# Expert rows in groups of 72 instead of 80 in a hybrid encoder step with 32 experts

## Chip, cores and metric

The kernel runs on one core of a Trainium2 chip. The metric is device time in microseconds of one launch. All data is float32.

## What is computed

One layer of a streaming encoder for 512 prompt tokens and 64 sample tokens, 576 rows of 1024 values: a mixer (SSD and S5 scans), cross attention over 256 memory tokens, and a mixture of experts. The change touches the last of these alone:

```python
def hmoe(x, p):
    """Two-level routing per token: top-1 expert group, then top-2 experts inside it."""
    t = x.reshape(bsz * L, D_MODEL)
    g_logits = (t @ p["w_router_group"]) + p["b_router_group"]
    g_idx = jnp.argmax(g_logits, axis=-1)
    ...
    top_v, top_i = lax.top_k(e_logits, TOP_K_INNER)
    gates = jax.nn.softmax(top_v, axis=-1) * g_prob[:, None]
    ...
    for e in range(N_EXPERTS):
        hid = jax.nn.silu(t @ p["w_gate"][e]) * (t @ p["w_up"][e])
        out = out + (hid @ p["w_down"][e]) * combine[:, e:e + 1]
```

There are 32 experts. Each has a gate and an up matrix of 1024 x 256 and a down matrix of 256 x 1024, 1 MB each. Each of the 576 tokens goes to two experts, so the experts have 1152 rows of work in all. Counted with the reference's routing on its inputs, the experts 0 to 31 get 18, 19, 9, 30, 20, 14, 25, 23, 28, 29, 29, 28, 31, 25, 33, 25, 52, 51, 32, 31, 62, 59, 33, 26, 49, 47, 46, 54, 46, 60, 52 and 66 rows.

## The kernel before

Every engine's program is written out by hand, with semaphores between the engines; nothing is scheduled by a tool. The mixer, the attention and the routing come first. Routing gives each row a rank within its expert (0, 1, 2 ...) and stores the normed rows in the DRAM tensor ffn_rows.

CAP = 80 is the number of row slots of an expert in one pass. The tile slot_id holds for each slot the rank that it takes, filled by GpSimd's iota in DEAL steps (lines 835 to 837):

```python
for turn_ in range(DEAL):
    step(pool.iota(iot[:, turn_:CAP:DEAL], [[1, CAP // DEAL]], base=turn_ * (CAP // DEAL), ...
```

With CAP = 80 and DEAL = 5, slots 0, 5, 10 ... 75 take ranks 0 to 15, slots 1, 6, 11 ... take ranks 16 to 31, and so on. One-hot tables made from it and a product over all tokens (slot_table, line 1377) give gather_index and scatter_index: for each slot and expert the token row to read, and the row of expert_rows to write. Empty slots get an index out of bounds, which moves no row. If an expert had more than CAP rows, overflow_flag would be set, and all engines would run further passes over all experts.

In the pass over the experts (lines named in the functions below), for expert n:
- **GpSimd** gathers the slots' rows into xg (region_r, two buffers, line 862) two experts ahead, once VectorE and TensorE have turned what the buffer held; and it scatters the finished rows yo (line 878). Both are indirect DMAs with CAP slots.
- **TensorE** turns half of xg by products with ident (turn_x, line 918 through turn), **VectorE** the other half (turn_half, line 2352), always in blocks of 32 rows up to 96. The result xgT is in region_t.
- **TensorE** computes gate and up (gate_up, line 1422): the weights are stationary, 64 columns at a time, and CAP columns of xgT stream. One expert has 128 instructions, 64 for each of gate and up. Then it turns the next expert's xg and computes the down product of the one before (down_rows, line 1438): hidden strips of 32, 32 and CAP - 64 rows are stationary, 256 columns of weights stream.
- **ScalarE** applies Silu (line 1801) and evicts (1796, 1809, 1810); **VectorE** multiplies to hidden (1854), and evicts (2379, 2380).
- **SyncE** loads weights (load_part, line 678). There are five sets of buffers for gate, up and down, spread over weight_ring, region_g, region_t, conv_io, act_a and act_b. All five are loaded ahead, during attention and routing. Each of the other 27 experts' sets is loaded into the buffers of the expert four before it: gate and up once that expert's up product is done, down once its down product is. Expert 31 takes the set of expert 0. All of this is one queue, in order.

At the end, each token's two rows are read back from expert_rows, added with their gates, normed and stored.

Of the kernel before, what the change touches and what calls it, by code (L numbers as in the profile page):

```python
# [42 lines left out]
CONV_OUT = CONV_COLS - 3  # L43
SAMPLE_COL = NP + 3
XC = [0, 128, 256, 384, SAMPLE_COL]
CAP = 80
DEAL = 5 if CAP % 5 == 0 else 4
DB = 32
XS = 96
PASSES = -(-T // CAP)  # L50
SETS = 5
# [166 lines left out]
def build(nc, a, o):  # L218
# [14 lines left out]
    with ExitStack() as ctx:  # L233
# [57 lines left out]
        def view(reg, off, *shape):  # L291
            n = 1
            for s in shape:
                n *= s
            v = reg[:, off:off + n]
            if len(shape) == 2:
                return v.rearrange("p (a b) -> p a b", a=shape[0])
            if len(shape) == 3:
                return v.rearrange("p (a b c) -> p a b c", a=shape[0], b=shape[1])
            if len(shape) == 4:  # L300
                return v.rearrange("p (a b c d) -> p a b c d", a=shape[0], b=shape[1], c=shape[2])
            return v
# [58 lines left out]
        xgT = [view(reg_t, XS * KD * i, KD, XS) for i in range(2)]  # L361
        gact = [view(reg_t, 2 * XS * KD + 160 * i, 2, CAP) for i in range(2)]
        hid = [rows[:, 1, 160 * i:160 * i + 2 * CAP].rearrange("p (j l) -> p j l", j=2) for i in range(2)]

# [17 lines left out]
        before = passing.take(NT, NE)  # L382
        oh = [passing.take(NT, CAP) for _ in range(2)]
        r_w = passing.take(NE)
# [9 lines left out]
        prio = lasting.take(NE)  # L394
        slot_id = lasting2.take(CAP)
        tok = [lasting2.take(NT, 2) for _ in range(2)]
# [2106 lines left out]
```

How the kernel before makes its waits and increments, by code:

```python
        def wait_filled(eng, *key):  # L484
            eng.wait_ge(filled, job[key] + 1)
            return bank_of(*key)
# [1 line left out]
        def wait_emptied(eng, *key):  # L489
            who, n = rank[job[key]]
            eng.wait_ge(emptied[who], n)
# [24 lines left out]
        def wait_chunk(eng, c):  # L517
            eng.wait_ge(ring_loaded[c % SLOTS], 16 * (c // SLOTS + 1))
# [43 lines left out]
        def wait_expert_chunk(eng, part, n, i, p):  # L563
            s = set_of(n)
            eng.wait_ge(WSEM[s][part], 16 * LOADS[s] * p + 16 * i + 16 * (WDENSE[s, part] + load_no(n) + 1))
# [1 line left out]
        def overflow_passes(eng, run_pass):  # L568
            eng.wait_ge(flag_ready, 1)
            over = eng.value_load(flag[0:1, 0:1], min_val=0, max_val=1)
            with eng.If(over > 0):
                with eng.Fori(1, PASSES) as p:
                    run_pass(p)
# [6 lines left out]
        @block.sync  # L581
# [47 lines left out]
            sp.dma_start(b_rt[:, 0:NG], a["b_router_group"].rearrange("o g -> (o g)").partition_broadcast(P))\  # L629
              .then_inc(route_loaded, 16)
            sp.dma_start(b_rt[:, NG:], a["b_router_expert"].rearrange("o g e -> (o g e)").partition_broadcast(P))\
              .then_inc(route_loaded, 16)
            sp.wait_ge(tap_ready, 1)
            sp.wait_ge(T_zero, 1)
            for k in range(8):
# [4 lines left out]
            for c in range(CH_GLU, CH_GLU + SLOTS):  # L641
                if c == CH_GLU + 4:
                    sp.wait_ge(h_ready, 1)
                    load_rows(5)
# [111 lines left out]
            def sync():  # L756
                pool.wait_ge(pstep, n[0])
```

## Time and profile before

| | us |
|---|---|
| median of 3 runs | 872.96 |
| the three runs | 869.98, 872.96, 873.88 |
| the profiled execution | 867.16 |
| its span, first to last instruction | 865.4 |

| stage of the profiled execution | us |
|---|---|
| mixer, attention, routing | 0 to 561.65 |
| gathers begin, experts | 561.65 to 829.1 |
| last scatter, reading back, final norm | to 865.4 |

The times come from one profiled execution; the hardware profiler records each instruction with its start and its duration. "Landing" is the time from the issue of a DMA to the semaphore that tells that its data is there. The DMA share is the mean over the 16 DMA engines of the time that their packets took; it can be a little over 1 where packets overlap.

### The profile page before, as it was taken

How to read it: one execution, taken by the hardware profiler on the slowest of the kernel's cores; microseconds unless marked ns; L12 is line 12 of the kernel's file. 1: busy time of each engine (PE TensorE's matmuls, PEld its weight loads, DVE VectorE, ACT ScalarE, POOL GpSimd, SP SyncE). 2: the span in 40 equal slices, each digit the busy share in tenths (PEclk: the TensorE clock that was granted, in tenths of full speed). 3: DMA queues.
4: the chain of work that ended last, by engine and by line, in shares of the span. 5: the costliest groups of instructions: out<-in, count | busy, mean ns of one | idle time of the engine just before them, and what ended most of it. 6: DMA issues, size and time to landing. Idle time of an engine off the chain costs nothing. (4 is left out here: it accounts for less than half of the span.)

```text
span 865.4 us, 21713 instructions
## 1 busy us (share of the span) xinstructions
PE 807.5 (93%) x9137; PEld 663.5 (77%) x9137; DVE 475.2 (55%) x1102; ACT 219.7 (25%) x497; POOL 144.6 (17%) x177
## 2 busy tenths in 40 slices
PE   5999999999999999999999999679999999999936
PEld 4778877877888888877888888567787887788722
DVE  2898997427351123310221455766677777777725
ACT  4402216435221101121221320222222222222213
POOL 1195100005220000000000000022232232233100
PEclk9999999999999999999999999689999999999977
DMA  9742174102212950061011252959999999999745
GB/s 261 231 121 40 22 181 146 50 13 101 93 55 73 311 187 1 19 224 50 1 49 49 73 189 80 373 198 369 379 401 401 397 404 381 397 397 389 287 139 214
DMA packets 76535, 167.61 MB, mean 194 GB/s; under 512 B 25712, under 2 KB 56560, under 8 KB 63616
## 3 DMA queue, kind: packets, MB, share of 16 engines
q1 hardware_dynamic: 61060, 151.45, 48.2%
q0 software_dynamic: 6144, 9.45, 3.3%
q10 hardware_dynamic: 9276, 5.93, 2.2%
q8 instruction: 40, 0.66, 0.3%
q14 instruction: 15, 0.12, 0.1%
HBM read 158.09 MB, written 17.88 MB: 203 GB/s over the span
## 5 line engine op out<-in xcount | busy, mean ns | idle before, releaser
L951 PE MATMUL bank<-act_a,weight_ring 128*128 128x288 f32 x768 | 190.8, 410 | 1.2 <-ACT act_a L1502 1.2
L951 PEld LDWEIGHTS bank<-act_a,weight_ring 128*128 128x128 f32 x768 | 146.2, 192 | 41.5 <-ACT act_a L1502 1.7
L2352 DVE STREAM_TRANSPOSE region_t<-region_r 32x128 f32<-32x128 f32 x372 | 151.3, 407 | 6.2
L1239 PE MATMUL bank<-weight_ring,act_b 128*128 128x256 f32 x512 | 111.8, 379 | 0.0
L1239 PEld LDWEIGHTS bank<-weight_ring,act_b 128*128 128x128 f32 x512 | 96.7, 190 | 12.9
L1854 DVE TENSOR_TENSOR region_u<-region_u,bank 128x512 f32<-128x512 f32 (+1 forms) x26 | 17.8, 686 | 90.3 <-PE bank L1239 66.4
L1422 PEld LDWEIGHTS bank<-region_t,weight_ring 128*64 128x64 f32 x1536 | 54.5, 139 | 4.7 <-issue 3.9
L1422 PE MATMUL bank<-region_t,weight_ring 128*64 128x80 f32 x1536 | 56.8, 233 | 1.4 <-issue 0.7
L1140 PE MATMUL bank<-weight_ring,region_u 128*128 128x256 f32 x256 | 56.6, 380 | 0.0
L1502 ACT ACTIVATE act_a<-bank 128x512 f32<-128x512 f32 (+1 forms) x46 | 22.7, 524 | 121.2 <-PE bank L918 94.1
L1140 PEld LDWEIGHTS bank<-weight_ring,region_u 128*128 128x128 f32 x256 | 48.4, 190 | 6.5
L843 POOL MEMSET region_r<- 96x1024 f32 x2 | 1.8, 948 | 262.1 <-PE bank L1308 262.1
L2321 DVE TENSOR_REDUCE score_max<-bank 128x2 f32<-128x512 f32 (+1 forms) x10 | 6.4, 636 | 67.1 <-PE bank L1281 63.3
L1422 PEld LDWEIGHTS bank<-region_t,region_g 128*64 128x64 f32 x1024 | 36.7, 138 | 4.7 <-issue 4.7
L1422 PE MATMUL bank<-region_t,region_g 128*64 128x80 f32 x1024 | 38.9, 234 | 1.1 <-issue 1.1
L878 POOL DMA_INDIRECT expert_rows<-region_r,scatter_now x32 | 30.1, 940 | 47.0 <-POOL scatter_now L873 24.7
L1809 ACT ACTIVATE region_r<-bank 32x256 f32<-32x256 f32 x64 | 24.2, 378 | 53.0 <-PE bank L1438 52.6
L918 PE MATMUL bank<-ident,region_r 80*128 80x80 f32 (+1 forms) x200 | 31.5, 286 | 5.4 <-DMA region_r<-ffn_rows,gather_index 4.3
L1796 ACT ACTIVATE region_t<-bank 128x320 f32<-128x320 f32 x32 | 14.0, 438 | 88.0 <-PE bank L918 88.0
L1854 DVE TENSOR_TENSOR row_stage<-region_t,bank 128x160 f32<-128x160 f32 x32 | 10.3, 321 | 46.0 <-PE bank L1422 46.0
L862 POOL DMA_INDIRECT region_r<-ffn_rows,gather_now x30 | 29.3, 977 | 25.9 <-POOL gather_now L856 25.9
L918 PE MATMUL bank<-ident,row_stage 128*128 128x128 f32 (+2 forms) x141 | 20.4, 295 | 13.8 <-DVE row_stage L1872 12.1
(353 smaller groups left out, 1171.7 us busy)
## 6 DMA issues: line engine op xcount, KB each, us to landing
weight_ring<-in_w_up SPq DMA_DIRECT2D x17, 1024.0 KB, 11.3
weight_ring<-in_w_down SPq DMA_DIRECT2D x10, 1024.0 KB, 9.5
weight_ring<-in_w_in SPq DMA_DIRECT2D x8, 1024.0 KB, 10.0
region_g<-in_w_up SPq DMA_DIRECT2D x8, 1024.0 KB, 11.5
region_g<-in_w_gate SPq DMA_DIRECT2D x8, 1024.0 KB, 9.5
conv_io<-in_w_gate SPq DMA_DIRECT2D x8, 1024.0 KB, 11.1
conv_io<-in_w_down SPq DMA_DIRECT2D x8, 1024.0 KB, 11.2
weight_ring<-in_w_gate SPq DMA_DIRECT2D x7, 1024.0 KB, 9.3
```

What stands on the lines that cost most here:

```text
L862: pool.indirect_dma_start(out=xg[b][0:CAP], out_offset=None, in_=xf_dram[:, :], in_offset=bass.IndirectOffsetOnAxis(ap=rows_now, axis=0), ...
L878: pool.indirect_dma_start(out=y2_dram[:, :], out_offset=bass.IndirectOffsetOnAxis(ap=cur_y[0:CAP, b:b + 1], axis=0), in_=yo[b][0:CAP], in_ ...
L918: return pe.transpose(out, in_, ident[0:m, 0:m])
L951: m = pe.matmul(ps[:, 0:HALF], slot(c)[:, k, P * (mt % 2):P * (mt % 2 + 1)], x[:, k, HALF * h:HALF * (h + 1)], start=(k == 0), stop=(k == ...
L1140: m = pe.matmul(ps[:, 0:CW], mnT[:, k, P * t:P * (t + 1)], slot(first_chunk + c)[:, k, :], start=(k == 0), stop=(k == KD - 1))
L1239: m = pe.matmul(ps[0:L, CW * cc:CW * (cc + 1)], x[:, k, t0:t0 + L], slot(c)[:, k, :], start=(k == 0), stop=(k == KD - 1))
L1422: m = pe.matmul(banks[2 + part][cols, CAP * j:CAP * (j + 1)], w[:, k, j::2][:, cols], xgT[b][:, k, 0:CAP], start=(k == 0), stop=(k == KD - 1))
L1502: act.activation(dst, src, func, scale=scale).then_inc(emptied["act"], 1)
L1796: act.activation(xgT[b][:, 4:8, 0:CAP], banks[b][:, 0:4 * CAP].rearrange("p (k l) -> p k l", k=4), ACT.Copy)\
L1809: act.activation(yo[b][DB * blk:DB * (blk + 1), 3 * CW:D], down_block(b, blk, 3), ACT.Copy)
L1854: return dve.tensor_tensor(out, x, y, op)
L2352: m = dve.transpose(xgT[b][DB * part:DB * (part + 1), 0:4, DB * blk:DB * (blk + 1)], xg[b][DB * blk:DB * (blk + 1), CW * part:CW * (part + 1)]
```

## The change

CAP becomes 72. DEAL follows from it and becomes 4, as 72 is not a multiple of 5.

```diff
@@ -43,7 +43,7 @@
-CAP = 80
+CAP = 72
 DEAL = 5 if CAP % 5 == 0 else 4
```

Slots 0, 4, 8 ... 68 now take ranks 0 to 17, slots 1, 5, 9 ... ranks 18 to 35, slots 2, 6 ... ranks 36 to 53, slots 3, 7 ... ranks 54 to 71. No instruction moves against another; their shapes change, and one iota goes. The number of passes that would be run in case of an overflow stays at eight in all.

On GpSimd, from the iotas to the first scatter, before:

```order
L836 IOTA iota_int 128x16 x5
L838 IOTA iota_int 128x5
L839 IOTA iota_int 128x5
L840 IOTA iota_int 128x32
L843 MEMSET region_r 96x1024 x2
L862 DMA region_r<-ffn_rows,gather_index 80x1024 x2
L856 COPY gather_now<-gather_index 80x1
L862 DMA region_r<-ffn_rows,gather_now 80x1024
```

and after:

```order
L836 IOTA iota_int 128x18 x4
L838 IOTA iota_int 128x5
L839 IOTA iota_int 128x5
L840 IOTA iota_int 128x32
L843 MEMSET region_r 96x1024 x2
L862 DMA region_r<-ffn_rows,gather_index 72x1024 x2
L856 COPY gather_now<-gather_index 72x1
L862 DMA region_r<-ffn_rows,gather_now 72x1024
```

Nothing moved: the DMAs stand where they stood, with 72 slots instead of 80.

On TensorE, at the beginning of the expert stage (turn, down product of expert 0, gate of expert 1), before:

```order
L918 MATMUL bank<-ident,region_r 128x80 x4
L1438 MATMUL bank<-weight_ring,row_stage 32x256 x2
L1438 MATMUL bank<-weight_ring,row_stage 16x256
L1438 MATMUL bank<-weight_ring,row_stage 32x256 x3
L1438 MATMUL bank<-weight_ring,row_stage 16x256
```

and after:

```order
L918 MATMUL bank<-ident,region_r 128x72 x4
L1438 MATMUL bank<-weight_ring,row_stage 32x256 x2
L1438 MATMUL bank<-weight_ring,row_stage 8x256
L1438 MATMUL bank<-weight_ring,row_stage 32x256 x3
L1438 MATMUL bank<-weight_ring,row_stage 8x256
```

The order is the same; the third strip has 8 rows instead of 16, and the turns stream 72 columns. The gate and up products (line 1422) go from 64x80 to 64x72 in the same way.

## Rows read from the trace of the kernel before

**Rows 1.** The page's span, and the granted clock in tenths in 40 slices of 21.6 us.
```profile
span 865.4 us, 21713 instructions
...
PEclk9999999999999999999999999689999999999977
```

**Rows 2.** Table of windows: busy time (instructions) per engine, granted clock, DMA share, GB/s.
```profile
626.00:818.00 192.00, 190.38 (x4321) 155.64 (x4321) 145.30 (x360) 50.20 (x120) 54.16 (x95) 1.00 1.01 392
```

**Rows 3.** DMA issues in 700:720 and 780:800: count, size, us to landing.
```profile
conv_io<-in_w_down SPq DMA_DIRECT2D x1, 1024.0 KB, 17.8
...
conv_io<-in_w_down SPq DMA_DIRECT2D x1, 1024.0 KB, 27.6
```

**Rows 4.** Timeline of SyncE's DMA issues: start us, us, line.
```profile
573.98 0.33 SPq L678 DMA_DIRECT2D region_t<-in_w_gate  x1
...
717.12 0.33 SPq L678 DMA_DIRECT2D conv_io<-in_w_down  x1
...
780.92 0.33 SPq L678 DMA_DIRECT2D conv_io<-in_w_down  x1
...
788.84 0.33 SPq L678 DMA_DIRECT2D weight_ring<-in_w_down  x1
...
790.04 0.33 SPq L594 DMA_DIRECT2D gain_rows<-in_norm_final  x1
```

**Rows 5.** DMA issues in 780:800, us to landing.
```profile
weight_ring<-in_w_down SPq DMA_DIRECT2D x1, 1024.0 KB, 29.0
...
gain_rows<-in_norm_final SPq DMA_DIRECT2D x1, 512.0 KB, 29.2
```

**Rows 6.** Timeline of TensorE: start us, us, line, form, [idle before <-releaser].
```profile
568.10 3.64 PE L1422 MATMUL bank<-region_t 128*64 128x80 f32 x64 [0.63 <-ACT region_t L1796]
...
809.71 2.80 PE L1438 MATMUL bank<-conv_io,row_stage 128*32 128x256 f32 x48
...
815.57 2.44 PE L1422 MATMUL bank<-region_t,weight_ring 128*64 128x80 f32 x64 [0.69 <-DMA weight_ring<-in_w_up]
...
818.54 2.80 PE L1438 MATMUL bank<-weight_ring,row_stage 128*32 128x256 f32 x48
```

**Rows 7.** The same: products with 72 columns at 87 us, with 80 at 797.
```profile
87.44 4.22 PE L1000 MATMUL bank<-region_u,region_t 128*64 128x72 f32 x128
...
91.59 0.65 PE L1012 MATMUL bank<-region_g,conv_io 128*32 128x128 f32 x16
...
796.62 2.44 PE L1422 MATMUL bank<-region_t,act_b 128*64 128x80 f32 x64
...
801.20 0.67 PE L918 MATMUL bank<-ident,region_r 80*128 80x80 f32 x4
```

**Rows 8.** Table of windows, early in the expert stage.
```profile
598.00:606.00 8.00, 7.80 (x176) 6.31 (x177) 5.22 (x14) 1.79 (x4) 1.36 (x3) 1.00 0.89 325
...
614.00:618.00 4.00, 2.86 (x72) 2.61 (x69) 1.37 (x5) 0.31 (x1) 0.94 (x1) 1.00 1.01 392
...
618.00:626.00 8.00, 7.82 (x181) 6.55 (x181) 5.97 (x15) 2.09 (x5) 2.30 (x4) 1.00 0.93 336
```

**Rows 9.** The page's part 3, GpSimd's DMA queue: packets, MB, share.
```profile
q0 software_dynamic: 6144, 9.45, 3.3%
```

**Rows 10.** Table of windows, end of the weight loads.
```profile
810.00:814.00 4.00, 4.00 (x92) 2.76 (x86) 3.44 (x10) 1.60 (x4) 0.00 (x0) 1.00 0.95 322
...
814.00:819.20 5.20, 4.51 (x106) 3.93 (x106) 2.95 (x8) 0.74 (x2) 1.11 (x2) 1.00 0.58 225
```

**Rows 11.** Timeline of GpSimd and VectorE in one expert, and landings of line 862.
```profile
677.95 0.98 POOL L862 DMA_INDIRECT region_r<-ffn_rows,gather_now  x1 [0.86 <-POOL gather_now L856]
...
686.13 2.51 DVE L2352 STREAM_TRANSPOSE region_t<-region_r 32x128 f32<-32x128 f32 x6
...
689.88 0.32 DVE L1854 TENSOR_TENSOR row_stage<-region_t,bank 128x160 f32<-128x160 f32 x1 [1.23 <-PE bank L1422]
...
DMA to landing us min/median/max: 2.5/7.4/7.9
```

## Prediction

> **What bounds the kernel now.** I read the expert stage first, as it is the only one that the change touches. It fills 568 to 829 us of a span of 865.4 [rows 1]. In the table of windows, TensorE is busy for 190.4 of the 192 us between 626 and 818 us, and this is what a reader sees first: it looks bound by TensorE. But the same row gives the 16 DMA engines a share of 1.01 at 392 GB/s [rows 2]. Both are full, and the landing times say which is the limit. SyncE issues the reload of a weight set as soon as TensorE frees it. The down weights that land in conv_io took 17.8 us from issue to landing for expert 21 and 27.6 us for expert 29 [rows 3]. A queue whose waiting time grows is asked for more than it can move. What keeps TensorE busy is the stock of five weight sets that were loaded ahead, and it is being used up. The end shows that it lasts just long enough: the last down weights were issued at 788.84 us [rows 4] and took 29.0 us [rows 5], so they landed at 817.8 us. TensorE had waited 0.69 us for the up weights of expert 30 at 815.57 and began its down product at 818.54 [rows 6], 0.7 us after the landing. So the stage ends with the DMA engines and TensorE level. The last 11 us of it (down of 30, all of 31) and the final stage stand behind that point.
>
> **Part 1: TensorE's products get shorter.** The gate and up products stream 80 columns, and then 72. One expert's 128 take from 796.62 to 801.20 = 4.58 us, 35.8 ns each. The same form with 72 columns is in the trace already, in an earlier stage: 128 of them from 87.44 to 91.59 = 4.15 us, 32.4 ns each [rows 7]. That is 0.43 us saved per expert. The down products stream 256 columns whatever CAP is; only a strip of 16 rows becomes one of 8: nothing. The four turns of xg take 0.67 us [rows 7]; ident streams 72 columns instead of 80, so I bound it by 0 and 10%, 0.07 us, and take 0. Over 32 experts that is 32 x 0.43 = 13.8 us of TensorE's time, 1.6% of the kernel, if TensorE were the limit.
>
> **Part 2: where that time goes.** From expert 5 on, expert n needs weights that are read at the DMA's pace: 27 reloads of 3 MB between the first issue at 573.98 [rows 4] and 817.8, 243.8 us or 9.0 us each, against the 7.97 us per expert on TensorE that are worked out below. The change does not alter one byte of them. The down weights of expert 21 were issued at 717.12 and landed at 734.9, those of expert 29 at 780.92 and 808.5 [rows 3, 4]. Eight experts in 63.8 us are 7.97 us each. Expert 29's down product began at 809.71 [rows 6], 1.2 us after the landing; expert 21's, 63.8 us earlier, had a margin of 11.0 us. The margin thus shrinks by 1.2 us per expert. With TensorE ahead by 0.43 n it is gone at 11.0 - 1.2 (n - 21) = 0.43 n, n = 22. So I expect the stock to be empty at expert 21 to 24 (735 to 760 us), and each later expert to wait for weights, some 9 us apart. The 13.8 us turn into waits. What is left of the gain is what moves the last landing, and what stands behind it:
> - The first reload waits for the gate and up products of expert 0, 568.10 to the issue at 573.98 us [rows 4, 6], a tenth shorter: -0.5 us.
> - While the queue was still short, the DMA engines idled a little: shares of 0.89 in 598 to 606 and 0.93 in 618 to 626 [rows 8] against 1.01, so 8 x (0.12 + 0.08) = 1.6 us. An earlier TensorE asks earlier and closes most of it: -1.5 us (bounds -0.9 and -1.6).
> - Behind the last up landing: expert 30's up products 0.2 us shorter, and expert 31's 0.43: -0.6 us.
>
> That is -2.6 us in all.
>
> **Part 3: rows per DMA engine.** A gather or a scatter has CAP slots; slots beyond an expert's count move no row. The page has 6144 packets on the GpSimd queue [rows 9]: 64 transfers of 96, which is 80 slots and one more for each of the 16 engines, which I read as five slots per engine. The deal in steps of five puts rank r in a slot of engine r mod 16. The reference's own routing on its inputs gives 9 to 66 rows per expert, 1152 in all (twice 1152 rows of 4 KB is 9.44 MB, the queue's 9.45 [rows 9]). Counting the transfers that fall among the reloads, gathers 3 to 31 and scatters 0 to 28, 2080 rows, the fullest engine gets 154, the emptiest 98, the mean is 130. Since every engine also carries a sixteenth of each weight load, the fullest one sets the last landing. The trace bears that out: before the last queued load landed (gain_rows, 790.04 + 29.2 = 819.2 us [rows 4, 5]) the share sank to 0.95 in 810 to 814 and 0.58 in 814 to 819.2 [rows 10]; the engines were on average done 4 x 0.06 + 5.2 x 0.43 = 2.5 us early. Divided by the 24 rows between fullest and mean this is 0.10 us per row. The other bound: the queue's 3.3% of 16 engines' span is 28.6 us per engine for 144 rows, 0.20 us each with all small packets [rows 9]. I take 0.12, nearer the tail, which measures just this.
>
> 72 slots cannot be cut in 16 equal shares, and no row of before shows how they are cut. If equal shares stay, as 80 has them, the number of engines must divide 72: 12 engines with 6 slots, or 8 with 9. With steps of four, ranks 0 to 17 stand in slots 0, 4, 8 and so on; a share of 6 slots has then two of them, the next share one. If the twelve rotate over the 16 in steps of 12, every other engine stays favoured: 177 rows on the fullest (8 by 9: 175). That is 23 more than now: +2.8 us (2.3 to 4.6). Other cuts give 130 to 139 (balanced) and 197 to 250 (piled up); they are the rivals. The 8 fewer empty slots per transfer have no price of their own in any row: at most the 0.07 us mean of all packets, 29 per engine, -2.1 us, at least 0; I take 0.
>
> The Trainium skill, "DMA: Bandwidth & Descriptors", section "Why a DMA increments its semaphore by 16 and not by 1", states that the descriptor generator takes the largest number of engines up to 16 that divides the slowest dimension, and on GpSimd's queue rotates over the engines when that is not 16. By it 72 rows use 12 engines, and the sum would be the one made here; the trace agrees for 80 slots (16 engines), and nothing in it shows 72. It also reports direct copies cut in shares of ceil(n/16), which would be the second rival.
>
> **Edits costed at nothing.** One iota fewer on GpSimd lies in its idle time before the stage; Silu, hidden and the evictions have 8 to 10% shorter operands beside TensorE. VectorE's 12 transposes always turn 96 rows. The gather is the one close cover: issued at 677.95, 7.4 us to landing, it is there at 685.4, and VectorE begins to turn that buffer at 686.13 [rows 11]. TensorE's two shorter experts take 0.9 us from the 1.9 us of slack up to the hidden product at 689.88. A landing slower by over 1 us would hold the experts back, but only below TensorE's own pace; as long as an expert takes less than the DMA's 9.0 us, nothing is lost at the end. That needs 4 us more per gather: costed at nothing.
>
> **The sum.** -0.5 - 1.5 - 0.6 + 2.8 = +0.2: no change. The profiled execution takes 867.2 us (span 865.4), and so I expect 867.4 for one like it; the runs shown have a median of 872.96, 5.8 us above, and I move the forecast from there: **873.2 us**. With all terms at their low ends (-0.5 - 1.6 - 0.6 + 2.3 - 2.1) it is 870.5, at their high ends (-0.5 - 0.9 - 0.6 + 4.6) 875.6.
>
> **The rivals.**
> - *Balanced rows.* If the cut leaves the fullest engine no fuller than now, -2.6 us: 870.4; if it comes out even, 24 rows fewer are a further -2.9: 867.5. For it: steps of four may happen to spread well, and the small packets are fewer. Against: 72 has no even cut. Chance 0.27.
> - *Piled-up rows, the slow side.* Shares of five from engine 0 on leave the 15th two slots and the last none: the fullest gets 197, +43 rows = +5.2, minus 2.6: 875.6, at 0.20 us per row 879.0. Twelve engines that are always the same would give 250 rows, +96 rows: 881.9 or more. It makes the kernel slower once the fullest engine has 2.6 / 0.12 = 22 rows more than now, and slower beyond 0.5% with about 58 at this price, or 35 at the dear one. Chance 0.22.
> - *TensorE is the bound after all*, and the queue's growth only reflects loads that are asked for too early: 13.8 us come back, 859.2. The row for it is the 99% busy TensorE; against it stand the growing landings and the 0.69 us wait. Chance 0.05.
> - *The clock falls.* If the waits for weights bring the granted clock down to its lower level (1.2 GHz, as at the start of the stage, where the page shows 6 tenths [rows 1], and where expert 0's gate products took 3.64 us instead of 2.44 [rows 6, 7]), the last eight experts take some 12 us instead of 9: +24, 897. Against it: the clock stayed at 1.00 with TensorE busy for 2.86 of 4 us at 614 to 618 [rows 8]. With whatever else I miss: 0.06.
> - *It does not fit in one pass.* An expert with over 72 rows would start seven more passes; the largest count is 66. Left at nearly nothing.
>
> **How the numbers follow.** The forecast's case has 0.40. The measurement tells about 0.5% (4.4 us) from no change: below 868.6 is faster, above 877.3 slower. Faster: TensorE as bound 0.05, some 0.11 of the balanced case. Slower: 0.16 of the piled-up case, 0.05 of the clock. So 0.16 faster, 0.63 same, 0.21 slower. The range reaches over the balanced case down to 867.3 (the even cut) and over the piled-up one with shares of five up to 879.0; outside stand the third and fourth rival and the same twelve engines, about 0.2.
>
> **What would show it.** Gate and up products of one expert in 4.15 us; experts 7.5 us apart up to about expert 22, and 9 us from there, with waits of TensorE for weights of 10 to 14 us in sum; landings that reach 27 us by 750 us; the last down weights at 816 to 820 us; the clock at 1.00. The packets on GpSimd's queue should be 64 x 88 = 5632. I am wrong in part 2 if the experts stay 7.5 us apart to the end, and in part 3 if the last landing moves by more than 5 us either way.

## The result, and the profile after

The changed kernel takes 882.96 us (median; 881.11 to 884.99), the kernel before on the same chip 872.95: a ratio of 1.0121, 95% interval 1.0087 to 1.0156. The change makes the kernel 10 us slower. The forecast was 873.2 us with a range up to 879.0. Every kernel time below is the median of its executions in the usual, faster state, and so is the time before that it is set against; the kernel with 96 slots in steps of four had one execution outside that state (908.95 us, at a lower clock), and with it its median is the 892.2 us that one expectation names.

The profiled execution took 885.0 us (span 883.3, against [rows 1]). TensorE's timeline of the kernel after (start us, us, line, form, idle before and its releaser), expert 0, expert 8, the first waits for weights (experts 19 and 20), and the end:

```profile
571.34 3.86 PE L1422 MATMUL bank<-region_t 128*64 128x72 f32 x64 [0.60 <-ACT region_t L1796]
...
640.03 2.23 PE L1422 MATMUL bank<-region_t,act_b 128*64 128x72 f32 x64
642.09 2.17 PE L1422 MATMUL bank<-region_t,act_a 128*64 128x72 f32 x64
644.19 0.66 PE L918 MATMUL bank<-ident,region_r 72*128 72x72 f32 x4
...
726.57 2.22 PE L1422 MATMUL bank<-region_t,weight_ring 128*64 128x72 f32 x64 [0.61 <-DMA weight_ring<-in_w_up]
...
733.99 2.23 PE L1422 MATMUL bank<-region_t,act_b 128*64 128x72 f32 x64 [1.88 <-DMA act_b<-in_w_gate]
...
832.69 2.23 PE L1422 MATMUL bank<-region_t,weight_ring 128*64 128x72 f32 x64 [0.45 <-DMA weight_ring<-in_w_up]
835.44 2.80 PE L1438 MATMUL bank<-weight_ring,row_stage 128*32 128x256 f32 x48
...
842.87 2.80 PE L1438 MATMUL bank<-weight_ring,row_stage 128*32 128x256 f32 x48 [0.48 <-DVE row_stage L1854]
```

One expert's gate and up products take 644.19 - 640.03 = 4.16 us, where [rows 7] had 4.58. From 726 us on TensorE waits for weights. Measured from expert 0's gate (571.34) to expert 31's down product (842.87), the stage takes 271.5 us; before it was 258.3, from 568.10 [rows 6] to

```profile
826.41 2.80 PE L1438 MATMUL bank<-weight_ring,row_stage 128*32 128x256 f32 x48 [0.49 <-DVE row_stage L1854]
```

Its start is 3.2 us later in this execution because the first stage took longer. That difference is between two executions: in the other profiles here the same gate starts anywhere between 566.8 and 573.6 us. So the two profiled executions lie 17.8 us apart and the medians 10; the 13.2 us of the stage are those of this pair.

The table of windows (busy us and instructions of PE, PEld, DVE, ACT, POOL; granted clock, DMA share, GB/s), kernel after:

```profile
626.00:818.00 192.00, 172.41 (x4078) 141.02 (x4078) 137.26 (x343) 45.89 (x112) 54.13 (x91) 1.00 1.02 379
...
640.00:810.00 170.00, 153.09 (x3604) 124.84 (x3600) 121.26 (x302) 41.75 (x102) 47.81 (x82) 1.00 1.02 378
...
822.00:826.00 4.00, 3.49 (x90) 3.13 (x86) 2.96 (x8) 0.70 (x2) 1.16 (x2) 1.00 0.81 260
826.00:830.00 4.00, 2.80 (x48) 1.71 (x49) 2.46 (x7) 1.35 (x3) 0.00 (x0) 1.00 0.46 174
830.00:834.00 4.00, 3.54 (x106) 3.41 (x107) 2.61 (x7) 0.29 (x1) 1.15 (x2) 1.00 0.41 151
834.00:838.00 4.00, 4.00 (x82) 2.76 (x78) 2.73 (x7) 0.96 (x3) 0.00 (x0) 1.00 0.11 43
```

and the kernel before in the same stretch:

```profile
640.00:810.00 170.00, 169.07 (x3844) 138.70 (x3844) 128.52 (x319) 44.11 (x106) 49.40 (x86) 1.00 1.02 395
```

TensorE gave up 16 of 170 us, and the clock stayed at 1.00. The DMA engines are as full as before (1.02), yet move 378 GB/s instead of 395. That is 4.3% of 170 us, or 7.3 us. Then, over the last 12 us before the last weights land, the share falls to 0.46 and 0.41. Before, 0.95 and 0.58 covered only 9 us [rows 10]. From 822 to 835 some 4 x 0.21 + 4 x 0.56 + 4 x 0.61 + 0.9 = 6.4 us of the mean engine are unused, against 2.5 before: 4 us more. Together these are 11 of the 13.2 us. The last queued load, gain_rows, landed at 805.52 + 31.4 = 836.9 us, where before it was 819.2 [rows 4, 5]:

```profile
805.52 3.20 SPq L594 DMA_DIRECT2D gain_rows<-in_norm_final  x1
...
gain_rows<-in_norm_final SPq DMA_DIRECT2D x1, 512.0 KB, 31.4
```

That is 17.7 us later, of which 3.2 are the later start. The prediction had named over 5 us as the sign that part 3 is wrong.

The page's part 3 gives the packets on GpSimd's queue, [rows 9] before:

```profile
q0 software_dynamic: 7168, 9.46, 3.5%
```

7168 is 64 x 112. I read this as six slots and one packet more for each of 16 engines, though there are only 72 slots. I had expected 5632.

### The profile page after: what moved, and what is told of

It is laid out like the page before. It is cut to its first block and busy times, and to the rows that moved or that the text cites. A ratio compares the mean times of both kernels' runs of the same rounds, so it can differ in the third digit from the quotient of the medians.

```text
span 883.3 us, 21712 instructions
## 1 busy us (share of the span) xinstructions
PE 801.3 (91%) x9137; PEld 656.3 (74%) x9137; DVE 474.5 (54%) x1102; ACT 218.6 (25%) x497; POOL 148.6 (17%) x176
## 3 DMA queue, kind: packets, MB, share of 16 engines
q0 software_dynamic: 7168, 9.46, 3.5%
## 5 line engine op out<-in xcount | busy, mean ns | idle before, releaser
L951 PE MATMUL bank<-act_a,weight_ring 128*128 128x288 f32 x768 | 193.0, 413 | 1.2 <-ACT act_a L1502 1.2
L1854 DVE TENSOR_TENSOR region_u<-region_u,bank 128x512 f32<-128x512 f32 (+1 forms) x26 | 17.8, 686 | 90.3 <-PE bank L1239 66.4
L1422 PEld LDWEIGHTS bank<-region_t,weight_ring 128*64 128x64 f32 x1536 | 49.7, 138 | 7.3 <-issue 4.0
L1422 PE MATMUL bank<-region_t,weight_ring 128*64 128x72 f32 x1536 | 52.1, 227 | 3.3 <-DMA weight_ring<-in_w_up 2.4
L1422 PEld LDWEIGHTS bank<-region_t,region_g 128*64 128x64 f32 x1024 | 33.4, 138 | 8.6 <-issue 4.9
L1422 PE MATMUL bank<-region_t,region_g 128*64 128x72 f32 x1024 | 35.6, 227 | 4.5 <-DMA region_g<-in_w_gate 2.8
L918 PE MATMUL bank<-ident,region_r 72*128 72x72 f32 (+1 forms) x200 | 31.2, 285 | 6.1 <-DMA region_r<-ffn_rows,gather_index 4.6
L1796 ACT ACTIVATE region_t<-bank 128x288 f32<-128x288 f32 x32 | 13.2, 411 | 87.7 <-PE bank L918 87.7
L918 PEld LDWEIGHTS bank<-ident,region_r 72*128 72x128 f32 (+1 forms) x200 | 25.3, 181 | 10.0 <-issue 6.3
## 6 DMA issues: line engine op xcount, KB each, us to landing
region_g<-in_w_up SPq DMA_DIRECT2D x8, 1024.0 KB, 19.1
```

The costliest lines, as they stand in the source:

```text
L918: return pe.transpose(out, in_, ident[0:m, 0:m])
L951: m = pe.matmul(ps[:, 0:HALF], slot(c)[:, k, P * (mt % 2):P * (mt % 2 + 1)], x[:, k, HALF * h:HALF * (h + 1)], start=(k == 0), stop=(k == ...
L1422: m = pe.matmul(banks[2 + part][cols, CAP * j:CAP * (j + 1)], w[:, k, j::2][:, cols], xgT[b][:, k, 0:CAP], start=(k == 0), stop=(k == KD - 1))
L1796: act.activation(xgT[b][:, 4:8, 0:CAP], banks[b][:, 0:4 * CAP].rearrange("p (k l) -> p k l", k=4), ACT.Copy)\
L1854: return dve.tensor_tensor(out, x, y, op)
```

## The experiments

Three theories run through the expectations. **F**: a transfer of 72 slots goes to the same 12 DMA engines each time, six slots each; 250 rows fall on the fullest. **R**: the twelve rotate over the 16, the first share going to the engine behind the last one of the transfer before; 177 rows. **P**: the packets cost, not the rows. "Fullest" counts the rows on one engine, as in the prediction, over gathers 3 to 31 and scatters 0 to 28. The kernel before has 154.

All kernels separate what CAP joined: CAP is now the computed columns alone, SLOTS_DMA the slots of gather, scatter and tables, and DEALT lists which slots take which ranks as (first slot, step, count, first rank, rank step):

```diff
-            for turn_ in range(DEAL):
-                step(pool.iota(iot[:, turn_:CAP:DEAL], [[1, CAP // DEAL]], ...
+            for s0, ds, cnt, base, dr in DEALT:
+                step(pool.iota(iot[:, s0:s0 + ds * (cnt - 1) + 1:ds], [[dr, cnt]], base=base, channel_multiplier=0))
```

Slots past CAP get rank 3000 and move nothing. The diffs below are against the kernel before, with this edit understood.

### First group: deals of 80 and of 72, and 72 columns in 80 slots

Rows in steps of ten instead of five, all else as before; fullest 245.

```diff
+SLOTS_DMA = 80
+DEALT = [(0, 10, 8, 0, 1), (1, 10, 8, 8, 1), (2, 10, 8, 16, 1), (3, 10, 8, 24, 1), (4, 10, 8, 32, 1), (5, 10, 8, 40, 1), (6, 10, 8, 48, 1), (7, 10, 8, 56, 1), (8, 10, 8, 64, 1), (9, 10, 8, 72, 1)]
```

> CAP stays 80 and the transfers keep 80 slots on 16 DMA engines; only the ranks are dealt in steps of ten, so that the fullest engine moves 245 rows among the reloads instead of 154. TensorE's work and the number of packets are those of before. Theory F (the fullest DMA engine sets the end, about 0.14 us per row; the 72 slots sit on the same twelve engines always, fullest 250): +91 rows, +12.7 us minus the 0.7 us that TensorE has in hand, 885 us (882 to 888). Theory P (it is the number of packets on GpSimd's queue, 7168 instead of 6144, that costs the time): packets unchanged, 873.

Measured 890.55 us, 1.0219 [1.0165, 1.0273]. That is 19.1 us for 91 rows more on the fullest engine, **0.21 us per row**. The windows show how it comes:

```profile
640.00:810.00 170.00, 157.29 (x3524) 128.86 (x3524) 119.48 (x298) 41.57 (x99) 45.37 (x80) 1.00 1.01 376
...
822.00:826.00 4.00, 3.78 (x80) 3.10 (x78) 2.32 (x6) 0.44 (x1) 0.00 (x0) 1.00 0.50 205
826.00:830.00 4.00, 3.53 (x86) 2.71 (x76) 3.09 (x9) 1.35 (x3) 1.54 (x4) 1.00 0.58 229
830.00:834.00 4.00, 3.97 (x88) 3.53 (x92) 1.99 (x6) 0.74 (x2) 0.95 (x2) 1.00 0.57 204
834.00:838.00 4.00, 2.85 (x64) 1.99 (x58) 3.38 (x9) 1.35 (x3) 0.23 (x1) 1.00 0.50 204
838.00:842.00 4.00, 3.92 (x108) 3.67 (x104) 1.28 (x4) 0.30 (x1) 0.89 (x2) 1.00 0.49 189
842.00:846.00 4.00, 4.00 (x74) 2.60 (x76) 3.38 (x9) 1.79 (x4) 0.00 (x0) 1.00 0.06 24
```

A deal in steps of ten over shares of five puts the low ranks on every second engine: eight get 210 to 245 rows, eight 22 to 43. For 20 us before the end the mean share is about one half (0.49 to 0.58), as if half of the DMA engines were done and half not. This is what "the fullest engine sets the end" of part 3 looks like. Ahead of it the rate is 376 GB/s at a share of 1.01, as in the kernel after.

72 slots dealt in steps of six; fullest 203 by F, 142 by R.

```diff
-CAP = 80
+CAP = 72
+SLOTS_DMA = 72
+DEALT = [(0, 6, 12, 0, 1), (1, 6, 12, 12, 1), (2, 6, 12, 24, 1), (3, 6, 12, 36, 1), (4, 6, 12, 48, 1), (5, 6, 12, 60, 1)]
```

> CAP 72 as in the changed kernel, but dealt in steps of six, so that each share of six slots gets ranks r mod 12. F, the same twelve engines always: fullest 203 instead of 250 rows, -47 x 0.14 = -6.6 us against the changed kernel, 876.4. Rotating twelve (theory R, the forecast's picture: fullest 177 before, 142 now; the 12.6 us lost against the forecast's -2.6 would then be 0.55 us per row): -35 rows, -19 us, 864. P: packets as in the changed kernel, 883.

Measured 875.65 us, 1.0055 [1.0031, 1.0079].

72 slots, ranks in slot order; fullest 348 by F, 175 by R, which is about that of the change.

```diff
+CAP = 72
+SLOTS_DMA = 72
+DEALT = [(0, 1, 72, 0, 1)]
```

> CAP 72 with the ranks in order of the slots (one step). F: the first engines get full shares of every expert, fullest 348 rows, +98 x 0.14 = +13.7 us against the changed kernel, 896.7. R: rotation evens this out, fullest 175 against 177: 883. P: 883.

Measured 892.58 us, 1.0259 [1.0203, 1.0315]. Only the deal differs between the changed kernel, e2 and e3, and their times are 883, 876 and 893 us (1.0121, 1.0055 and 1.0259 of before, each on its own chip). So the deal matters, and P alone falls (all three have 7168 packets). R alone falls too: it gives the change and e3 the same fullest engine, and they are 9.6 us apart (12 by the ratios).

72 columns computed, 80 slots moved; fullest 171.

```diff
-CAP = 80
+CAP = 72
+SLOTS_DMA = 80
+DEALT = [(0, 5, 15, 0, 1), (1, 5, 15, 15, 1), (2, 5, 14, 30, 1), (3, 5, 14, 44, 1), (4, 5, 14, 58, 1), (72, 1, 8, 3000, 1)]
```

> TensorE, ScalarE and VectorE work on 72 columns, but gathers and scatters keep 80 slots (the last eight always empty), dealt in steps of five over the 72: 16 engines, fullest 171 rows, 96 packets per transfer as before. F: 873 - 2.6 (what the shorter products leave) + 17 x 0.14 = 872.8. P: packets as before, so only -2.6: 870.4. If the shorter products themselves slowed the stage, it would stay near 883.

Measured 872.85 us, 1.0017 [0.9986, 1.0047]. Nearly the whole loss is gone, with the short products kept: this interval ends below the one of the change (from 1.0087). **The 72 slots of the transfers cost the 10 us; the 72 columns neither cost nor gain anything that can be told from noise.** Its window has TensorE at 161 us, not 153, and the rate is back:

```profile
640.00:810.00 170.00, 160.85 (x3815) 131.14 (x3811) 128.38 (x320) 43.25 (x106) 48.45 (x85) 1.00 1.02 393
```

### Second group: the limit lifted, and a sure set of twelve

Both kernels with only a quarter of each down matrix read on a reload, which takes a quarter off the reloads' bytes; the rest of those weights is left from the expert before in the set.

```diff
+                    if part == 2:
+                        sp.dma_start(WSET[set_of(n)][2][:, 0:512], experts_of[2][bass.ds(BODY * i + n, 1), :, 0:512]
...
```

> CAP 80, but every reload of a down matrix brings only its first 512 of 2048 columns, a quarter, so the experts from 5 on use partly old down weights; TensorE's work is unchanged. The DMA engines then need some 6.8 us per expert instead of 9.0. If the DMA engines and TensorE are level in the kernel before, only the 0.7 us wait and its 0.7 us margin go: 871 to 872.

> The changed kernel (CAP 72, steps of four) with the same quarter of the down matrices on reload. If the shorter products are worth 0.43 us per expert wherever the DMA is no limit, this is 13 to 14 us below the kernel with CAP 80 and the same light loads: 858, 25 us below the changed kernel. If the turns or the gathers became the limit, it stays above 864.

Measured 869.04 us with 80 (0.9979 [0.9951, 1.0008]) and 858.34 us with 72 (0.9856 [0.9805, 0.9907]), 10.7 us apart. Windows of 80, then of 72:

```profile
640.00:810.00 170.00, 169.08 (x3854) 138.53 (x3844) 129.25 (x321) 44.99 (x108) 49.61 (x87) 1.00 0.88 318
```

```profile
640.00:810.00 170.00, 169.08 (x4088) 139.00 (x4084) 136.31 (x339) 45.66 (x112) 53.20 (x90) 1.00 0.89 321
```

With the DMA engines at 0.88 and 0.89, TensorE is the bound and the short products pay: 4088 instructions in the same 169 us instead of 3854. They pay 10.7 of the 13.8 us counted in part 1. And a quarter fewer bytes gave the kernel before 2.1 us (at most 4.3, by the interval): it stands where both limits meet. The second of these kernels is the change itself with fewer bytes, slots of 72 included: the edit that costs 10 us with all bytes gains 10.7 us with a quarter fewer.

72 columns in 96 slots, steps of four: six slots on each of 12 engines for certain, and empty slots on four; fullest 250.

```diff
-CAP = 80
+CAP = 72
+SLOTS_DMA = 96
+DEALT = [(0, 4, 18, 0, 1), (1, 4, 18, 18, 1), (2, 4, 18, 36, 1), (3, 4, 18, 54, 1), (72, 1, 24, 3000, 1)]
```

> 72 columns for the engines and the deal in steps of four, but the gathers and scatters have 96 slots, of which the last 24 are always empty: six slots on each of 16 engines. If 72 slots are cut in shares of six for the same twelve engines, and the other four get empty packets, this has the same rows on each engine and the same 112 packets, and takes the changed kernel's 883 us within 0.5%. If the twelve rotate, it is slower than the changed kernel. If the cut is another one, it differs.

Measured 890.35 us, 1.0219 [1.0157, 1.0282]; 7168 packets, as in the changed kernel. This is what F says the change does, and it is 7.4 us slower than the change by the times, 8.5 by the ratios; the two intervals just miss each other (1.0156 and 1.0157). So F, too, doesn't hold as it stands.

72 columns in 80 slots, every second step dealt backward; fullest 145.

```diff
+CAP = 72
+SLOTS_DMA = 80
+DEALT = [(0, 5, 15, 0, 1), (1, 5, 15, 29, -1), (2, 5, 14, 30, 1), (3, 5, 14, 44, 1), (4, 5, 14, 71, -1), (72, 1, 8, 3000, 1)]
```

> 72 columns for the engines, 80 slots for the transfers, and the five steps of the deal run forward and backward over the engines in turn, so that the fullest of the 16 moves 145 rows instead of 171 with steps all forward. F: 26 rows x 0.12 us (the price between the runs with 171, 203 and 348 rows) = -3.1 us against that kernel's 872.9: 869.7, 3 us below before. P: 872.9.

Measured 871.25 us, 1.0005 [0.9979, 1.003]. With 26 rows fewer than e4 this is 1.0 us less by the ratios (1.6 by the times, on two chips), where 0.21 us per row would give 5.5. The kernel has all the gains of part 2 and 9 rows fewer than before on the fullest engine: by the forecast's terms -2.6 - 9 x 0.12 = -3.7 us. It measured +0.4 us (-1.8 to +2.6, by the interval).

### Third group: the price of a packet, and balanced rows

72 columns in 96 slots, ranks in slot order; fullest 348 for certain.

```diff
+CAP = 72
+SLOTS_DMA = 96
+DEALT = [(0, 1, 72, 0, 1), (72, 1, 24, 3000, 1)]
```

> 72 columns, transfers of 96 slots, ranks in order of the slots: shares of six on 16 engines that are surely the same each time, fullest 348 rows. The kernel with 72 slots and the same deal took 892.6 us. If its twelve engines are always the same, this one takes the same, 892 to 895. If they rotate (as the 9 us between the kernel with 96 slots in steps of four, 892.2, and the changed kernel, 883.0, suggest), this one is well above: 348 - 250 = 98 rows more than the 892.2 us kernel, at 0.21 us each (91 rows cost 19.0 us in the kernel with steps of ten), 913.

Measured 900.9 us, 1.0343 [1.0298, 1.0389], neither of the two times expected. 98 rows more than e9 cost 10.6 us by the times and 10.8 by the ratios, 0.11 each. e3, which F equates with it, has 892.58.

80 columns in 96 slots, balanced to 155 on the fullest: as before, but with 16 more packets per transfer and all of them empty.

```diff
+SLOTS_DMA = 96
+DEALT = [(0, 6, 14, 13, -1), (1, 6, 14, 14, 1), (2, 6, 13, 40, -1), (3, 6, 13, 41, 1), (4, 6, 13, 66, -1), (5, 6, 13, 79, -1), (80, 1, 16, 3000, 1)]
```

> TensorE works on 80 columns as before, but transfers have 96 slots (the last sixteen empty) and so 112 packets instead of 96; the deal runs forward and backward over shares of six so that the fullest engine has 155 rows, as before's 154. Only the number of packets differs from before. Theory P's part: the weight packets took 340 to 347 ns on average in all kernels with 112 packets and 332 in the balanced ones with 96; 9 ns x 648 packets per engine = 6 us, 877. If rows on the fullest engine are all that counts: 871 to 872.

Measured 873.27 us, 1.0028 [1.0, 1.0055]: 2.8 us beside the kernel before's 870.48, 0 to 4.8 by the interval, so at the edge of what can be told. The packets may not be all of it, as the rows lie otherwise, too: 13 engines have 148 to 155, one 99 and two none. Such packets can be some 2.8 of the change's 10 us. They don't explain the lower rate ahead of the end, which is 390 GB/s here with 7168 packets, and was 376 in e1 with 6144:

```profile
640.00:810.00 170.00, 167.95 (x3819) 137.58 (x3817) 128.81 (x319) 44.67 (x107) 49.75 (x86) 1.00 1.01 390
```

80 columns in 80 slots, balanced; fullest 135.

```diff
+SLOTS_DMA = 80
+DEALT = [(0, 5, 16, 0, 1), (1, 5, 16, 31, -1), (2, 5, 16, 32, 1), (3, 5, 16, 48, 1), (4, 5, 16, 79, -1)]
```

> CAP 80 and 80 slots as before; the five steps of the deal run forward and backward in turn, so that the fullest engine has 135 rows instead of 154 (mean 130). If the fullest engine alone set the last landing, TensorE would be left as the bound with its 0.7 us wait and 0.7 us margin: 870.0, 1.4 us below before. If before is already at the rate of all 16 engines together, no difference: 871.4.

Measured 867.83 us, 0.9974 [0.9949, 0.9999].

### Fourth group: who gets the first slots, and can 80 be beaten

The kernel before, and behind its last store four series of 16 scatters into a scratch tensor, rows of 16 KB, a few valid rows in the first slots:

```diff
+            for turn_, (n_slots, n_rows) in enumerate(((72, 6), (80, 5), (96, 6), (72, 6))):
+                for k in range(16):
+                    pool.indirect_dma_start(
+                        out=probe_dram[:, :], out_offset=bass.IndirectOffsetOnAxis(ap=probe[0:n_slots, k:k + 1], axis=0),
...
+                pool.wait_ge(probe_done, 256 * (turn_ + 1))
```

> The kernel before, and behind its last store four series of 16 scatters with no weight traffic beside them, each transfer with a few rows of 16 KB in its first slots and nothing else: 72 slots with 6 rows, 80 slots with 5 rows, 96 slots with 6 rows, 72 slots with 6 rows again. If the first slots are always one engine's (theory F), the rows of a series follow each other on that engine at some 0.6 us each (twice an 8 KB packet): 16 x 6 x 0.62 = 60 us for 72 slots, 50 us for 80, 60 us for 96. If the twelve engines of a 72-slot transfer rotate (theory R), its rows fall on four engines in turn and the series is done when it has been issued, in some 17 to 25 us, with 80 and 96 slots still at 50 and 60 us.

The instructions of each series (duration ns min/median/max, first and last start) and the longest time to a landing, for 72, 80, 96 and 72 slots in turn:

```profile
L914 POOL DMA_INDIRECT probe_rows<-region_r,probe_index x16: 925/935/968, 869.9 to 888.5; - x16
...
DMA to landing us min/median/max: 3.2/3.2/33.9
...
L914 POOL DMA_INDIRECT probe_rows<-region_r,probe_index x16: 902/907/930, 923.2 to 941.4; - x16
...
DMA to landing us min/median/max: 3.1/3.1/32.7
...
L914 POOL DMA_INDIRECT probe_rows<-region_r,probe_index x16: 907/912/915, 974.9 to 993.2; - x16
...
DMA to landing us min/median/max: 3.1/3.1/42.5
...
L914 POOL DMA_INDIRECT probe_rows<-region_r,probe_index x16: 925/932/947, 1036.5 to 1055.0; - x16
...
DMA to landing us min/median/max: 3.2/3.2/33.9
```

From the first start to the last landing: 72 slots 888.5 + 33.9 - 869.9 = 52.5 us, 80 slots 50.9, 96 slots 60.8, 72 again 52.4. Between 80 and 96 slots lie 16 rows and 9.9 us, 0.62 us per row, so both have all their rows on one engine. With 72 slots the series takes 52.5 us, where F wanted 60 and R under 25. The page's rate, in 40 slices of the 54 us of the first series and of the 63 us of the third, shows the rest:

```profile
GB/s 0 12 25 25 37 37 25 12 37 49 37 25 49 49 25 37 49 49 24 36 49 24 36 24 24 24 36 24 24 24 24 36 24 24 24 24 36 24 24 0
```

```profile
GB/s 10 0 32 21 21 31 21 31 31 21 31 21 32 21 31 31 21 31 21 31 21 31 31 21 31 21 31 31 21 31 21 31 31 21 31 21 31 21 31 10
```

With 96 slots the rate is that of one engine, 21 to 32 GB/s, from end to end. With 72 it is often 37 to 49 up to the middle, and about 25 from there: a second engine helped for a while.

The single packets of the trace tell how much. The first series has 96 packets of 16 KB. Followed from the end of one to the start of the next, they form two chains, one of 72 packets and one of 24. The second chain comes in four groups of six, and the first of them starts 4.2 us after the first packet, when the fourth transfer has been issued (873.65 - 869.88 = 3.8 us). The last series of 72 slots has the same: 72 and 24, from 4.2 us on. So of 16 transfers, 12 gave their first share to one engine and four to another. A packet takes 0.61 us alone and up to 1.57 us while two run at once (21.7 of 50.5 us), which is why the chain of 72 lasts longer than 72 x 0.61 = 44 us.

One theory fits that, call it **L**: a transfer of 72 slots takes the next twelve engines as in R, but its first share goes to the lowest-numbered of the twelve. In steps of 12 over 16, four sets of twelve take turns; three of them contain engine 0, which then gets the first share, and the fourth does not. Counted over the deals, with the first transfer beginning at any of the 16 engines, L gives the change 183 to 192 rows on the fullest engine, e2 148 to 157 and e3 258 to 264. The prices come from other kernels: 2.8 us for packets (e11), 0.21 us per row up to e1's 245 rows, 0.11 above.

| | rows by L | L, us | R, us | F, us | measured, us |
|---|---|---|---|---|---|
| change | 183 to 192 | +8.9 to 10.8 | +7.6 | +22 | +10.0 |
| e2 | 148 to 157 | +1.5 to 3.4 | +0.3 | +13 | +4.2 |
| e3 | 258 to 264 | +23.3 to 24.0 | +7.2 | +33 | +21.1 |

L is within 3 us of all three; R misses e3 by 14 us, F misses all three by about 9 us or more. The engines' numbers themselves are not in the trace, so L is what fits the probe and the kernels, not something read off.

77 columns in 80 slots, fullest 135, beside e8's kernel again:

```diff
-CAP = 80
+CAP = 77
+SLOTS_DMA = 80
+DEALT = [(0, 5, 16, 0, 1), (1, 5, 16, 31, -1), (2, 5, 15, 32, 1), (3, 5, 15, 47, 1), (4, 5, 15, 62, 1), (77, 1, 3, 3000, 1)]
```

> 77 columns computed instead of 80 (the fullest expert has 77 or fewer rows), transfers of 80 slots, rows dealt forward and backward in turn so that the fullest engine has 135 rows. If the stretch is bound by the weights' bytes and the rows on the fullest engine, three columns fewer give nothing: as e14, within 0.2%. If TensorE still has a part in it, a twenty-fifth off each product gives up to 1 to 2 us: 0.995 of before.

> 80 columns and 80 slots, dealt forward and backward so that the fullest engine has 135 rows instead of 154: 0.997 of before, some 2 to 3 us less, if a row on the fullest engine costs 0.12 to 0.15 us.

Measured 870.37 us (0.9986 [0.996, 1.0012]) and 869.14 us (0.9991 [0.9965, 1.0016]). They are the same, as the bound by weights says. Over its two measurements the balanced deal of 80 gains 0.1 to 0.3%, at the edge of what can be told. The windows of the second at the end have 0.98 in 814 to 818 us and 0.11 behind, where the kernel before has 0.71 and 0.07: the 16 engines now finish together, but hardly earlier.

```profile
814.00:818.00 4.00, 4.00 (x119) 3.91 (x114) 2.87 (x7) 0.34 (x2) 1.11 (x2) 1.00 0.98 393
818.00:822.00 4.00, 4.00 (x73) 2.61 (x73) 3.29 (x9) 1.79 (x4) 0.00 (x0) 1.00 0.11 42
```

## Why the prediction was wrong, by its own steps

**The bound, right.** The growing landings and the 0.69 us wait were the sign; TensorE at 99% was not. e5 and e6 show it: the change gains 10.7 us with a quarter fewer bytes. With all of them the short products gain nothing (e4, e7).

**Part 1, right.** 4.16 us per expert against 4.15 predicted.

**Part 2, right in kind, its gain not seen.** Experts were to be 7.5 us apart up to about expert 22, and then 9, waiting for weights. From expert 8's gate (640.03 us) to expert 19's (723.73) they are 7.6 us apart, from expert 20's (733.99) to expert 30's (830.02) 9.6. The first waits are at 726.57 us (expert 19) and 733.99 (expert 20), as the queue fell behind faster than reckoned. TensorE's waits for weights sum to 13.7 us (10 to 14 predicted); the largest sums (us, times, longest) are

```profile
PE bank L1422 <- DMA act_b<-in_w_gate: 4.6, 3, 1.9
PE bank L1422 <- DMA region_g<-in_w_gate: 2.8, 3, 1.0
PE bank L1422 <- DMA weight_ring<-in_w_up: 2.4, 4, 0.7
PE bank L1422 <- DMA act_a<-in_w_up: 1.6, 3, 0.7
```

The gains of 0.5, 1.5 and 0.6 us beside it can't be read apart, and their sum of 2.6 us is not seen: e4 and e7 have them all and lie at 1.0017 and 1.0005 of before, and e7's interval leaves at most 1.8 us of gain where the forecast's terms give 3.7. Why is open. The DMA share in 598 to 606 us rose from 0.89 to 0.94 and in 618 to 626 from 0.93 to 0.99, as against [rows 8], which is the way that the 1.5 us needs, but these windows lie 3.2 us earlier in the stage than before's:

```profile
598.00:606.00 8.00, 8.00 (x192) 6.25 (x187) 5.85 (x15) 2.08 (x6) 0.97 (x1) 0.96 0.94 340
...
618.00:626.00 8.00, 6.43 (x142) 5.04 (x140) 4.76 (x13) 2.02 (x5) 1.06 (x3) 1.00 0.99 351
```

**Part 3, the step that failed.** +2.8 us were predicted for the cut of 72, with 4.6 at the high end. The slots of 72 cost some 9 us against e4 with the same columns, and the kernel got 10 us slower. That the uneven rows on the DMA engines decide was right; three sizes were off:
- *The price of a row.* I took 0.12 us, from the unused DMA time at the end of the loads, as "the tail measures just this"; the other bound was 0.20. e1 gives 0.21, close to that other bound. The tail shows only the lead that the emptier engines have at the very end. In e1 that lead is some 22 us between eight engines with 210 to 245 rows and eight with 22 to 43, about 190 rows or 0.12 us per row, near the tail's price of before. But the emptier engines finished no sooner than before (their share drops at 818 us in an execution 4 us late), though they carried some hundred rows fewer than the mean of 130. The rest of the price lies ahead of the tail, as 376 to 379 GB/s instead of 395 (e1, the change, e9), at an unchanged share. Why packets take longer there is not shown; one reason would be that the emptier engines can only be as far ahead as loads are queued, and no run tests it. The price isn't constant: in the range from 135 to 171 rows it is 0.04 to 0.15 us (e4 to e7, e8 and e14 against before; of these only e8's is clear of nothing, and just so), and above 250 it is 0.11.
- *The fullest engine.* 177 by an even rotation, where L has 183 to 192. F's 250 stood in the second rival, at 881.9 us or more; the time agrees with that figure, but by luck: e9 has 250 rows for certain and takes 890.
- *The packets.* Costed at nothing to -2.1 us for 8 fewer empty slots. There were 16 more packets, not 8 fewer, and e11 prices them at +2.8 us (0 to 4.8).

With the measured sizes the sum is 29 to 38 rows x 0.21 = 6.1 to 8.0 and 2.8 for packets, 8.9 to 10.8 us. None of these is taken from the change's own time. But the sum leaves out part 2's -2.6 us, and the packets' price has an interval from 0 to 4.8, so it agrees with the 10 us without proving each term.

**The rule of the Trainium skill.** I had weighed the Trainium skill, "DMA: Bandwidth & Descriptors", section "Why a DMA increments its semaphore by 16 and not by 1", and had written that by it the sum would be my own. That was a misreading. The Trainium skill states, in that section, that such a transfer takes consecutive engines from a cursor that goes round, as in R, but also that its first share goes to the lowest-numbered of them, which is L. The trace's 112 packets agree with shares of six, and the probe's 72 and 24 packets agree with this clause and speak against the even rotation that I took from it. With the whole rule the forecast's own price would have given 29 to 38 rows x 0.12 = 3.5 to 4.6 us instead of 2.8: the misreading is the smaller part of the miss, the price of a row the larger.

**The costs put at nothing.** The gather: I said a landing slower by 1 us would hold the experts back. VectorE did wait for gathers, 8.5 us in 11 waits where line 862 before had none:

```profile
L862 POOL DMA_INDIRECT region_r<-ffn_rows,gather_now x30: 1022/1030/1039, 572.5 to 820.0; - x30
...
  DVE region_t L2352: 8.5, 11
```

No wait of TensorE is put down to these transposes, so they seem covered, as foreseen, by the waits for weights; no run took the two apart. **The rivals.** TensorE as bound: no. The falling clock: not where it was feared, as it is 1.00 in all windows from 618 us on. But it fell once early in the stage, for 3.4 us:

```profile
594.00:598.00 4.00, 3.85 (x43) 2.32 (x47) 1.29 (x4) 0.59 (x2) 1.40 (x3) 0.66 1.02 382
```

The kernel before kept 1.00 there. TensorE had just been idle for 1.48 us, up to 594.15. e4 has the same fall at the same place and not the loss. One pass sufficed.

## What to carry to other kernels

When TensorE is busy but the time from issue to landing grows from load to load, shortening its work gives nothing: lift the other limit in an experiment (here a quarter of the bytes) before paying for the edit. The number of rows in an indirect transfer is a choice of its own, separate from the number computed; spread the valid rows evenly over the DMA engines, which is easy to count when it is a multiple of 16, since beside a full weight queue each 4 KB row on the fullest DMA engine cost up to 0.21 us. A multiple of 16 alone does not help: 96 slots filled unevenly cost 19 and 30 us (e9, e10). The price read from the tail of the queue (0.10 to 0.12 us) was half of the measured one, because the rate ahead of the tail fell as well. And a rule of the Trainium skill is to be read to its end: the clause left out here was the one that makes the rotation uneven.

## Unexpected in the hardware

- A transfer of 72 slots made as many packets as one of 96 (112), and its GpSimd instruction was longer than with 80: 1030 ns at the median against 976. It is not the packets that make it longer, as with 96 slots it was 983 (e9). Sixteen empty packets more per transfer cost 0.04 us each time (2.8 us over 64 in e11, at the edge of noise).
- A 72-slot transfer used changing engines, but not evenly: of 16 transfers 12 gave their first share to the same engine. Beside each other, two engines' packets of 16 KB from the same six partitions took up to 1.57 us instead of 0.61.
- Where the weight queue is deep, SyncE's issue instructions of line 678 themselves grow, from 0.33 us [rows 4] to 3 us, in the kernel after:

```profile
716.37 1.02 SPq L678 DMA_DIRECT2D conv_io<-in_w_down  x1
...
731.07 3.20 SPq L678 DMA_DIRECT2D weight_ring<-in_w_up  x1
...
801.51 3.05 SPq L678 DMA_DIRECT2D weight_ring<-in_w_down  x1
```

Loads issued from 716 to 802 us took 32 to 36 us to land.
